# DeltaNet scan: state products, decay sums, differences and exponentials at earlier levels, the first inverse built on GpSimd

## What is computed

```python
g = jnp.cumsum(g.reshape(B, H, N, C), -1)
decay = jnp.where(incl, jnp.exp(jnp.where(incl, g[..., :, None] - g[..., None, :], 0.0)), 0.0)
a = jnp.where(strict, jnp.einsum('bhnid,bhnjd->bhnij', kb, k) * decay, 0.0)
t_inv = lax.linalg.triangular_solve(eye + a, jnp.broadcast_to(eye, a.shape), left_side=True, lower=True, unit_diagonal=True)
v_new = u_i - jnp.einsum('bhck,bhkv->bhcv', w_i, s)
s_next = s * gl_i[..., None, None] + jnp.einsum('bhck,bhcv->bhkv', kd_i, v_new)
o = jnp.einsum('bhck,bhkv->bhcv', qd_i, s) + jnp.einsum('bhij,bhjv->bhiv', at_i, v_new)
```

## Time and profile before

| | us |
|---|---|
| median of the runs | 2786.13 |
| lowest and highest of three | 2785.48, 2788.02 |
| the profiled execution | 2802.93 |
| its span | 2801.2 |
| busy in the span: PE, PEld | 2514.6 (90%), 2179.1 (78%) |
| busy: DVE, ACT, POOL | 1802.1 (64%), 1556.8 (56%), 795.3 (28%) |

### The profile page before, as it was taken

One profiled execution on the slowest core, in us unless ns is written; L12 is line 12 of the kernel. 1 busy time (PEld: TensorE's weight loads), 2 busy tenths in 40 slices (PEclk: granted clock), 3 DMA queues, 4 the chain that ended last, 5 costly groups with the idle time before them and its releaser, 6 DMA issues. The chain is left out here.

```text
span 2801.2 us, 135939 instructions
## 1 busy us (share of the span) xinstructions
PE 2514.6 (90%) x57273; PEld 2179.1 (78%) x57273; DVE 1802.1 (64%) x2076; ACT 1556.8 (56%) x1972; POOL 795.3 (28%) x607
## 2 busy tenths in 40 slices
PE   8999997889888875999989999999998999999993
PEld 2444555889887544998989898888888999999993
DVE  2434896767765776254363755877777876778883
ACT  3521553444445535164464655777777766677773
POOL 1202103556553112122131322222322232323321
PEclk9999998999999986999999999999999999999997
DMA  9500001100002228256383856988888977889975
GB/s 366 208 31 31 3 1 31 32 23 22 28 25 78 86 90 328 79 190 222 95 316 85 327 175 236 370 311 310 318 319 321 326 265 285 309 292 335 345 257 199
DMA packets 124489, 536.93 MB, mean 192 GB/s; under 512 B 12540, under 2 KB 13552, under 8 KB 91616
## 3 DMA queue, kind: packets, MB, share of 16 engines
q1 hardware_dynamic: 107120, 481.80, 45.7%
q0 software_dynamic: 14464, 47.79, 7.7%
q10 hardware_dynamic: 2832, 6.37, 0.6%
HBM read 496.99 MB, written 38.92 MB: 191 GB/s over the span
## 5 line engine op out<-in xcount | busy, mean ns | idle before, releaser
L2378 PE MATMUL ps<-qkv,weights 128*128 128x64 f16 x10496 | 941.2, 193 | 65.8 <-issue 33.2
L2378 PEld LDWEIGHTS ps<-qkv,weights 128*128 128x128 f16 x10496 | 921.8, 98 | 81.4 <-issue 46.8
L2379 PE MATMUL ps<-qkv,weights 128*128 128x64 f16 x10496 | 940.1, 193 | 3.7 <-issue 3.5
L2380 PE MATMUL ps<-qkv,weights 128*128 128x64 f16 x10496 | 940.1, 193 | 1.7 <-issue 1.0
L2380 PEld LDWEIGHTS ps<-qkv,weights 128*128 128x128 f16 x10496 | 923.2, 98 | 5.0 <-issue 5.0
L2379 PEld LDWEIGHTS ps<-qkv,weights 128*128 128x128 f16 x10496 | 923.3, 98 | 2.9 <-issue 2.9
L1827 DVE SCALAR_TENSOR_TENSOR weights<-hT,weights 128x2048 f16<-128x2048 f16 (+1 forms) x256 | 586.4, 2343 | 167.2 <-ACT weights L1254 138.5
L1254 ACT ACTIVATE weights<-hT 128x2048 f16 (+1 forms) x256 | 527.4, 2102 | 80.2 <-DMA hT<-in_w_gu_dram 58.6
L2395 PE MATMUL ps<-qkv,weights 128*128 128x64 f16 x5248 | 477.5, 193 | 26.7 <-DVE weights L1832 22.3
L2395 PEld LDWEIGHTS ps<-qkv,weights 128*128 128x128 f16 x5248 | 461.2, 98 | 35.0 <-DVE weights L1832 27.9
L2396 PE MATMUL ps<-qkv,weights 128*128 128x64 f16 x5248 | 477.1, 193 | 2.3 <-issue 1.9
(11 more groups left out here) (421 smaller groups left out, 4361.4 us busy)
## 6 DMA issues: line engine op xcount, KB each, us to landing
hT<-in_w_gu_dram SPq DMA_DIRECT2D x256, 1024.0 KB, 10.2
qkv<-in_w_down_dram SPq DMA_DIRECT2D x128, 1024.0 KB, 5.8
weights<-in_w_ada_dram SPq DMA_DIRECT2D x12, 2048.0 KB, 15.2
qkv<-in_w_in_dram SPq DMA_DIRECT2D x4, 2048.0 KB, 7.9
hT<-decay_rows SPq DMA_DIRECT2D x20, 256.0 KB, 3.3
hT<-beta_rows SPq DMA_DIRECT2D x20, 256.0 KB, 3.3
qkv<-in_x_dram ACTq DMA_DIRECT2D x8, 512.0 KB, 6.7
weights<-in_w_in_dram SPq DMA_DIRECT2D x2, 2048.0 KB, 13.8
```

The lines of the kernel that those rows point to most:

```text
L2378: pe.matmul(dst, ghi[k][:, b, c], xT[:, 0, k, :], start=first, stop=False, skip_group_check=True)
L2379: pe.matmul(dst, ghi[k][:, b, c], xT[:, 1, k, :], start=False, stop=False, skip_group_check=True)
L2380: last = pe.matmul(dst, glo[k][:, b, c], xT[:, 0, k, :], start=False, stop=end, skip_group_check=True)
```

## The change

The state products and their taking off move to level 1, both sums to level 2, the differences to levels 2 and 3, the exponentials to levels 3 and 4. On GpSimd the staging of the next decays moves to level 1 and the decayed queries to level 2. The addition of the identity moves from VectorE to GpSimd, right behind each mask of the first block. The low half of the first inverse is made direction by direction ahead of that direction's output (`first_low`). ScalarE makes the high half of the first inverse before it copies the turned one, and TensorE turns the keys before the first inverse.

```diff
--- before.py
+++ after.py
@@ -777,6 +777,7 @@
             e_g.ahead(pool)
             e_st.ahead(pool)
             e_B.ahead(pool)
+            e_T.ahead(pool)
             e_qd.ahead(pool)
 
             def stage_decays(s, out, ahead):
@@ -813,6 +814,11 @@
                     e_P.before(pool, s, 2 * (NL - 1) + r, ahead)
                     pool.sem_inc(s_idle, 1)
                     masked(r, 0)
+                    e_B.now(pool, s, r, ahead)
+                    e_u.before(pool, s, r, ahead)
+                    pool.sem_inc(s_idle, 1)
+                    pool.tensor_tensor(dn[r]["tT"], dn[r]["b0"], ident[:].unsqueeze(1).to_broadcast([P, H, P]),
+                                       ALU.add).then_inc(e_T.sem, 1)
 
             def first():
                 stage_decays(0, False, 0)
@@ -830,7 +836,7 @@
                             e_P.before(pool, s, 2 * (NL - 1 - l) + r)
                         pool.sem_inc(s_idle, 1)
                         masked(r, l)
-                    if l == 1:
+                    if l == 2:
                         for r in range(DIRS):
                             if out:
                                 e_D.now(pool, s, r)
@@ -840,7 +846,7 @@
                                 pool.tensor_tensor(dn[r]["qd"], dn[r]["qc"], dn[r]["eg"], ALU.mult).then_inc(e_qd.sem, 1)
                             else:
                                 pool.sem_inc(e_qd.sem, 1)
-                    if l == 2 and more:
+                    if l == 1 and more:
                         stage_decays(s, next_out, 1)
                 if more:
                     stage_chunk(s, next_out, 1)
@@ -1109,12 +1115,12 @@
 
             def inverses_and_keys(s, ahead):
                 for r in range(DIRS):
+                    e_T.now(act, s, r, ahead)
+                    act.activation(tTh[r][:, 0], dn[r]["tT"], ACT.Copy, scale=TSCALE).then_inc(e_Th.sem, 1)
+                for r in range(DIRS):
                     e_X.now(act, s, r, ahead)
                     act.activation(dn[r]["t"], bank(r, 2), ACT.Copy).then_inc(e_Xc.sem, 1)
                 for r in range(DIRS):
-                    act.activation(tTh[r][:, 0], dn[r]["tT"], ACT.Copy, scale=TSCALE).then_inc(e_Th.sem, 1)
-                for r in range(DIRS):
-                    e_Q.now(act, s, r, ahead)
                     for h in range(H):
                         last = act.activation(dn[r]["kdec"][:, h, :], bank(r, 0)[:, h, :], ACT.Copy,
                                               scale=ge[:, r, 8 + h:9 + h])
@@ -1147,8 +1153,8 @@
                             e_TP.now(act, s, 2 * (l - 1) + r)
                             act.activation(d["tT"], bank(r, 1), ACT.Copy,
                                            scale=1.0 / (TSCALE * TSCALE)).then_inc(e_F.sem, 1)
-                    if more and 4 <= l < 4 + DIRS:
-                        exponentials(s, l - 4, next_out, 1)
+                    if more and 3 <= l < 3 + DIRS:
+                        exponentials(s, l - 3, next_out, 1)
                 for r in range(DIRS):
                     d = dn[r]
                     e_u.now(act, s, r)
@@ -1541,7 +1547,7 @@
             dve.sem_inc(s_zero, 1)
             for r in range(DIRS):
                 link(dve.memset(dn[r]["state"], 0.0))
-            for e in (e_E, e_A, e_T, e_Pl, e_Tl, e_R, e_S):
+            for e in (e_E, e_A, e_Pl, e_Tl, e_R, e_S):
                 e.ahead(dve)
 
 
@@ -1567,18 +1573,13 @@
                     link(dve.tensor_tensor(d["aT"], d["aT"], d["decay"], ALU.mult))
                     e_K.now(dve, s, r, ahead)
                     dve.tensor_tensor(d["aT"], d["aT"], bank(r, 2), ALU.mult).then_inc(e_A.sem, 1)
-                for r in range(DIRS):
-                    d = dn[r]
-                    e_B.now(dve, s, r, ahead)
-                    e_u.before(dve, s, r, ahead)
-                    dve.tensor_tensor(d["tT"], d["b0"], ident[:].unsqueeze(1).to_broadcast([P, H, P]),
-                                      ALU.add).then_inc(e_T.sem, 1)
+
+            def first_low(s, r, ahead):
+                e_Th.now(dve, s, r, ahead)
+                dve.scalar_tensor_tensor(tTh[r][:, 1], dn[r]["tT"], TSCALE, tTh[r][:, 0], ALU.mult,
+                                         ALU.subtract).then_inc(e_Tl.sem, 1)
 
             def values(s, out, ahead):
-                for r in range(DIRS):
-                    e_Th.now(dve, s, r, ahead)
-                    dve.scalar_tensor_tensor(tTh[r][:, 1], dn[r]["tT"], TSCALE, tTh[r][:, 0], ALU.mult,
-                                             ALU.subtract).then_inc(e_Tl.sem, 1)
                 for r in range(DIRS):
                     d = dn[r]
                     e_Q.now(dve, s, r, ahead)
@@ -1592,6 +1593,8 @@
                 for r in range(DIRS):
                     decays(0, r, 0)
                 matrix(0, 0)
+                for r in range(DIRS):
+                    first_low(0, r, 0)
                 values(0, False, 0)
 
             def step(s, out, more, next_out):
@@ -1616,21 +1619,23 @@
                             e_Th.now(dve, s, 2 * l + r)
                             dve.scalar_tensor_tensor(low, half_bank(r, 1, l), 1.0 / TSCALE, high, ALU.mult,
                                                      ALU.subtract).then_inc(e_Tl.sem, 1)
-                    if 2 <= l < 2 + DIRS:
-                        r = l - 2
-                        d = dn[r]
-                        e_ws.now(dve, s, r)
-                        for h in range(H):
-                            last = dve.scalar_tensor_tensor(d["vb"][:, h, :], bank(r, 3)[:, h, :], bg[:, r, h:h + 1],
-                                                            d["vb"][:, h, :], ALU.mult, ALU.add)
-                        last.then_inc(e_R.sem, 1)
-                    if more and 4 <= l < 4 + DIRS:
-                        decays(s, l - 4, 1)
+                    if l == 1:
+                        for r in range(DIRS):
+                            d = dn[r]
+                            e_ws.now(dve, s, r)
+                            for h in range(H):
+                                last = dve.scalar_tensor_tensor(d["vb"][:, h, :], bank(r, 3)[:, h, :], bg[:, r, h:h + 1],
+                                                                d["vb"][:, h, :], ALU.mult, ALU.add)
+                            last.then_inc(e_R.sem, 1)
+                    if more and 2 <= l < 2 + DIRS:
+                        decays(s, l - 2, 1)
                 if more:
                     matrix(s, 1)
                 for r in range(DIRS):
                     d = dn[r]
                     o = o_at[r]
+                    if more:
+                        first_low(s, r, 1)
                     e_o.now(dve, s, r)
                     if out:
                         link(dve.tensor_tensor(o, o, bank(r, 1), ALU.add))
@@ -2114,14 +2119,14 @@
 
             def turns(s, out, ahead):
                 for r in range(DIRS):
+                    for h in range(H):
+                        pe.transpose(bank(r, 0)[:, h, :], dn[r]["kc"][:, h, :], ident[:])
+                for r in range(DIRS):
                     d = dn[r]
                     e_T.now(pe, s, r, ahead)
                     for h in range(H):
                         last = pe.transpose(bank(r, 2)[:, h, :], d["tT"][:, h, :], ident[:])
                     last.then_inc(e_X.sem, 1)
-                for r in range(DIRS):
-                    for h in range(H):
-                        pe.transpose(bank(r, 0)[:, h, :], dn[r]["kc"][:, h, :], ident[:])
                 for r in range(DIRS):
                     d = dn[r]
                     e_S.before(pe, s, r, ahead)
@@ -2183,12 +2188,13 @@
                             last = pe.matmul(turned[:, h], pr[:, 1, h, :], tcol[0][:, h], start=False, stop=h == H - 1,
                                              skip_group_check=True)
                         last.then_inc(e_TP.sem, 1)
-                    if l == 2:
+                    if l == 1:
                         for r in range(DIRS):
                             d = dn[r]
                             heads(bank(r, 3), lambda h: d["kc"][:, h, :], lambda h: d["state"][:, h, :]).then_inc(e_ws.sem, 1)
-                    if more and 3 <= l < 3 + DIRS:
-                        sums(s, l - 3, 1)
+                    if more and l == 2:
+                        for r in range(DIRS):
+                            sums(s, r, 1)
                 for r in range(DIRS):
                     d = dn[r]
                     e_R.now(pe, s, r)
```

## The result

| | before | after |
|---|---|---|
| median us (lowest, highest; six runs each) | 2786.33 (2785.02, 2789.74) | 2800.07 (2793.84, 2801.82) |
| ratio, 95% interval | | 1.0044, 1.0030 to 1.0057 |
| the profiled execution, its span | 2802.93, 2801.2 | 2801.82, 2800.1 |

The changed kernel is slower by 13.7 us (0.5%), where I had forecast 1.4. The time is inside the range and beyond the likeliest case's own range (2778 to 2797). The two profiled executions can't be set against each other as wholes: that of before was 0.6% above its median, that of after 0.1%. Outside the scan that of before took 12.0 us more than that of after (2368.9 and 2356.9 us). The scan can be compared. I mark each step by ScalarE's first copy of the new values (L1156 before, L1162 after); the first interval counts from SyncE's first transfer of the scan (L590, at 452.14 and 450.97 us).

A forecast was written before the change was run, and what follows sets the result against it. TensorE's waits, chiefly 3.25 us at level 5 for ScalarE's late copy, and its low clock were taken as the bound. Per chunk -6.7 and +7.05 gave +0.35; with the other steps +1.3 on 2786.13, about 2787.5 us; range 2758 to 2808.

The forecast's parts named there:

- the likeliest case's own range: 2778 to 2797 us around the 2787.5 forecast, chance 0.50, from an uncertain 0 to 2.0 us and the clock's 1.7 to 2.7.
- The price that decides: Differences at levels 2 and 3: each short VectorE instruction meeting a GpSimd mask takes 1.3 us; level 3 waits +3.7 us.
- The mark that I had named: Sign in the profile after: L1558 at 1 us or more on average, instead of 0.33 to 0.65.
- The first two rivals: Mask costs what a copy costs, 0.65 us per instruction: 2763, chance 0.22. No contention, 0.28 us: 2739, chance 0.04.
- The price of the low clock: After the level 3 wait TensorE's clock falls again, costing +2.4 us a chunk, as it did before the change.
- levels 4 and 5: Second differences meeting masks 6: 0 to 2.0 us, taken as +0.6, more if clock returns early; exponentials before L1133: +0.35.
- Start of a chunk: Identity addition on GpSimd costs nothing, values come earlier, the 0.59 us level 1 wait goes: -0.85 us a chunk.
- State products at level 1: Moving them one level costs nothing: they keep 1.87 us and cover VectorE's taking off of the state's part.
- queues passed: GpSimd's reordered masks, queries and decay staging: masks 3 just in time, decay rows with 0.5 us to spare, no cost.
- The 0.2 us before u: Saving from the 3.39 us between keys' product and u, as exponentials no longer stand ahead of L1136.
- Steps 0 and 1 and the first chunk: Outside the steady steps: about +1.1 us for step 0, -1.1 for step 1, -0.3 for the first chunk.
- The slower rival: Second TensorE wait of 2 to 3.3 us, clock low to level 6, if it passes 2.03 us: 2805, chance 0.24.

The follow-up runs named there:

- experiment 1: Changed kernel, with TensorE writing the triangular mask to PSUM, so the differences' short VectorE instructions have one tensor in SBUF: 2737.01 us, ratio 0.9816 to the kernel before.
- experiment 2: Changed kernel, with the four short difference instructions of a direction replaced by two long ones of 512 columns: 2785.69 us, ratio 0.9994 to the kernel before.
- experiment 8: The kernel of experiment 1, with the identity added on VectorE again instead of GpSimd: 2756.53 us, ratio 0.9851 to the kernel before.
- experiment 9: The kernel of experiment 1, with the first chunk's identity additions on VectorE and the context steps' low halves behind both state updates: 2747.15 us, ratio 0.9808.
- 10: The kernel of experiment 1 run again unchanged, on the same chip as experiment 9: 2746.50 us, ratio 0.9808 to the kernel before.
- experiments 3 and 4: Changed kernel with unread TensorE filler products: first 28 at level 3 (2849.58 us, ratio 1.0229), then 15 at level 3 and 14 at level 4 (2810.24 us, 1.0033).
- experiment 6: Kernel before the change, with the triangular mask and the sums read from PSUM: 2778.01 us, ratio 0.9925.
- experiment 7: The kernel of experiment 1, with sums, differences and exponentials back at their old levels: 2779.47 us, ratio 0.9917 to the kernel before.
- experiment 5: Changed kernel, with sums, differences and exponentials back at their old levels: 2796.92 us, ratio 1.0028 to the kernel before.

## Why the prediction was right or wrong

**The price that decides** held. I took 1.3 us for each L1558 beside a mask; the first three took 1.43, 1.34 and 1.35 us, L1555 (L1561 now) took 1.01, the fourth L1558 some 0.3, and TensorE's wait at level 3 is 3.44 us for a forecast of 3.7. The mark that I had named, 1 us or more on average, is reached by these quartets (1.06) but not by the line as a whole (0.68), since direction 1's run alone. The Trainium skill, "SBUF — State Buffer", section "Who interferes with whom", says that a VectorE instruction with two SBUF inputs contends with a GpSimd instruction that reads SBUF, that one with at most one SBUF input (outside the modes with two ports) does not, and that the contention is an exclusive lock. By that rule, the trace agrees on all three: with one input moved to PSUM four instructions beside masks fell from 4.23 to 1.11 us (experiment 1), and in experiment 2 either engine waited for the other. The first two rivals fall by it: a mask does not cost what a copy costs (2763), and there is contention (2739).

**The price of the low clock** was the step that failed in the steady chunk. I took +2.4 from the earlier trace rows on the ground that a longer wait than 3.25 us brings the same. It brought 4.3, since the clock stayed low for 9.3 us, where it had been low for 6 before. Against that, **levels 4 and 5** cost nothing: the second differences found no mask in their way and the exponentials stood in nobody's, so +0.6 and +0.35 go. In all 3.44 + 4.3 for 3.7 + 2.4 + 0.6 + 0.35, 0.7 us more. Step 2 went as the text on level 4 had it for an early clock (a second wait, 0.58 us), and was faster, not slower: 41.08 us, though 1.5 us of that are no work of the clock.

**Start of a chunk** was undersized: -0.85 was forecast. From u to level 3 took 21.61 us before and takes 21.11, although the sums of 0.89 us now stand in it: -1.4. The 0.59 us wait is gone as said. **State products at level 1** and **queues passed** cost nothing, as said: no wait of TensorE for a mask of level 3, and the decayed queries and decay rows came in time. The 0.2 us before u came as well (3.18 us for 3.39). So the steady step adds up as -1.4 - 3.25 - 2.4 - 0.2 + 7.7 = +0.5 us, for +0.35 forecast: two errors of 0.5 and 0.7 that nearly cancel, and that is luck.

**Steps 0 and 1 and the first chunk** are where the prediction missed the time: +1.1, -1.1 and -0.3 forecast, +10.4 measured. Three things were wrong in it. First, I priced the addition on GpSimd by when it is done, and not by the clock behind it. Up to level 1 the first chunk even gains 0.7 us; but TensorE then takes 5.89 us for level 1 at the low clock, where it took 3.44, and experiment 8 against 1 and experiment 9 against 10 give 3.3 to 3.5 us for the additions on GpSimd; in the first of these pairs 2.7 of it are clock. Second, I moved the low half in front of the output product without looking at a step that has no output, where direction 1's then stands behind direction 0's state update (1.73 us in step 1). Third, I expected the differences of step 1 to be free. Those of direction 0 are (four L1564 in 1.13 us), in step 0 as well; but those of direction 1 meet the masks of level 6 and the copies of the next chunk (L1561 1.28 us, four L1564 3.27 us), and TensorE waits at level 4, 3.64 us in step 0 and 3.32 in step 1. The clock of 0.50 behind it costs step 0 most, for it had been 1.00 there behind 2.03 us; in step 1 it had been low before too. By the rows of TensorE the +6.0 us of the first interval are -0.7 up to level 1, +3.3 from there to level 3 (0.9 of it the sums, the rest clock) and +3.4 from level 3 to u. The +4.3 of step 1 are +0.9 up to level 1, +2.9 to level 3 (0.9 of it the sums), +2.0 in levels 3 to 5 and -1.4 from level 6 to u.

**The slower rival** named a second idle stretch and a low clock through level 5, 2805 us. The time came out nearer to it (2800) than to the forecast, but not by its mechanism: in the steady steps the clock is low into level 5 after a single wait. The wait at level 4 is real: as a second wait it stands in experiments 3 and 4 (3.3 us) and in step 2 (0.58), and alone in steps 0 and 1. Its point of decision, that an idle stretch must pass 2.03 us, is refuted by experiments 6 and 7, where 1.38 us was enough in some steps.

**The ledger**: the scan of the two profiled executions accounts for 10.9 of the 13.7 us between the medians; the other 2.8 lie within what executions of one kernel differ by. That the time fell into the range is owed to the range: of its centre the steady steps were right by two errors, and the steps of the context were 10.7 us off.

## What to carry to other kernels

Before a VectorE instruction is moved, look at what GpSimd does at the new place: with two inputs in SBUF, each short instruction there can cost its partner's length (1.3 us beside a mask here), and once it cost six partners (experiment 5), so count instructions and not columns. A small constant operand can be written to PSUM by TensorE for one product, and here that turned a change of +0.4% into one of -1.8%. Price a moved step in the first and in the odd iterations by their own rows; the steady one says nothing of them.

## What was unexpected of the hardware

- An instruction of VectorE with 4 columns and both inputs in SBUF was passed by six GpSimd copies in a row, 3.19 us (experiment 5), while others of the same line alternated with masks at 1.01 and 1.28 us. What decides between the two was not tried.
- The length of an idle stretch does not tell here whether the clock falls, nor for how long. Behind the same 1.38 us of idle time it fell in two of six like steps of experiment 6 and in five of six of experiment 7 (not at 697.84 us, with a granted clock of 1.00 from 698 to 704), and it did not fall behind 2.03 us in step 0 of the kernel before. Behind the same wait of 2.7 us it was low for some 10 us in one step of experiment 2 and for some 3 in another, and the steps differed by 2.8 us.
